# Hybrid attention block: output product fed by transposed raw rows, norms applied on the way out

## The reference, cut to what matters

```python
proj = rms_norm(x, attn_norm) @ w_in
y_nsa = rms_norm(nsa_mixer(...), nsa_out_norm)        # 512 columns, one root per token
o = rms_norm(o, out_gain) * silu(g)                   # HGRN: 4 heads of 128, one root per token and head
x = x + concatenate([y_nsa, y_hg]) @ w_out
h = rms_norm(x, mlp_norm)                             # 1024 columns, one root per token
x = x + square(relu(h @ w_mlp_in)) @ w_mlp_out
```

## Time and profile before

| | us |
|---|---|
| median of 3 runs | 1640.95 |
| range of the runs | 1636.74 to 1642.53 |
| the profiled execution, its own time | 1642.76 |
| its span, first to last instruction | 1640.9 |
| TensorE busy | 1543.2 (94%) |
| VectorE busy | 727.7 (44%) |
| ScalarE busy | 397.9 (24%) |
| GpSimd busy | 423.3 (26%) |
| mean granted TensorE clock | 0.978 |

### The profile page before, as it was taken

The page is one execution under the profiler, slowest core; times in us unless marked ns, Lnnn a source line. Parts: engine busy times, 40 slices in busy tenths (PEclk is TensorE's granted clock), DMA queues, the critical chain, the costliest instruction groups (busy, mean ns, idle before and its releaser), DMA issues.

```text
span 1640.9 us, 24059 instructions
## 1 busy us (share of the span) xinstructions
PE 1543.2 (94%) x8345; PEld 1316.1 (80%) x8345; DVE 727.7 (44%) x1324; ACT 397.9 (24%) x890; POOL 423.3 (26%) x427
## 2 busy tenths in 40 slices
PE   3999998989999999989799699999999999999998
PEld 3988887878888888879688588888888888888886
DVE  5001852016666666689701634444334444334334
ACT  5012311124545454532701411111100111111110
POOL 1333331320000000000323053334444443334411
PEclk9999999998999998999999899999999999999999
DMA  4211130100000000040011021111111111111102
GB/s 151 58 52 45 52 91 24 39 6 1 2 0 0 0 0 0 0 149 2 27 39 59 19 65 45 46 52 52 51 51 51 51 49 47 45 51 51 45 20 103
DMA packets 44690, 69.30 MB, mean 42 GB/s; under 512 B 5688, under 2 KB 23648, under 8 KB 44640
## 3 DMA queue, kind: packets, MB, share of 16 engines
q1 hardware_dynamic: 42368, 67.78, 13.4%
q10 hardware_dynamic: 2272, 0.84, 0.2%
HBM read 64.41 MB, written 4.19 MB: 42 GB/s over the span
## 4 chain that ended last, share of the span: by engine, by line
PE 87%; DVE 8%; ACT 3%; issue 2%; ACTq 0%; DVEq 0%
PE ps L425 65%; PE ps L1517 7%; PE ps L1477 4%; PE ps L1492 4%; PE ps L1540 2%; DVE hT_low L484 1%; PE ps L1511 1%; PE ps L1461 1%; PE ps L1375 1%; PE ps L1482 1%; DVE hgrn_k L1214 1%; PE ps L558 1%; DVE mixed_rows L1303 1%; DVE x L1332 1%; DVE hgrn_q L1213 0%
## 5 line engine op out<-in xcount | busy, mean ns | idle before, releaser
L425 PE MATMUL ps<-hT_high,w_high 128*128 128x512 f32 x640 | 249.1, 389 | 1.4 <-DVE hT_low L484 1.4
L425 PE MATMUL ps<-hT_high,w_low 128*128 128x512 f32 x640 | 249.0, 389 | 0.0
L425 PE MATMUL ps<-hT_low,w_high 128*128 128x512 f32 x640 | 249.0, 389 | 0.0
L1332 DVE TENSOR_TENSOR x<-ps,x 128x512 f32<-128x512 f32 x256 | 171.1, 688 | 97.0 <-PE ps L425 97.0
L742 POOL CAST w_high<-w_raw 128x512 fp32r<-128x512 f32 x128 | 91.6, 716 | 447.5 <-PE ps L425 385.8
L425 PE MATMUL ps<-w_high,hidden_high 128*128 128x512 f32 x512 | 199.4, 390 | 1.6 <-DVE x L1332 1.6
L425 PE MATMUL ps<-w_low,hidden_high 128*128 128x512 f32 x512 | 199.2, 389 | 0.0
L425 PE MATMUL ps<-w_high,hidden_low 128*128 128x512 f32 x512 | 199.2, 389 | 0.0
L1314 DVE TENSOR_TENSOR relu_squared<-relu 128x512 f32<-128x512 f32 x64 | 49.2, 791 | 322.3 <-ACT relu L970 322.3
L970 ACT ACTIVATE relu<-ps 128x512 f32<-128x512 f32 x64 | 38.4, 600 | 589.4 <-PE ps L425 587.9
L744 POOL TENSOR_TENSOR w_low<-w_raw,w_high 128x512 fp32r<-128x512 f32 x128 | 174.5, 1363 | 10.2
(11 more groups left out here) (175 smaller groups left out, 2237.1 us busy)
## 6 DMA issues: line engine op xcount, KB each, us to landing
w_raw<-in_w_mlp_in_dram SPq DMA_DIRECT2D x64, 256.0 KB, 2.7
w_raw<-in_w_mlp_out_dram SPq DMA_DIRECT2D x64, 256.0 KB, 2.8
w_raw<-in_w_in_dram SPq DMA_DIRECT2D x48, 256.0 KB, 2.7
x_in<-in_x_dram SPq DMA_DIRECT2D x8, 512.0 KB, 8.8
w_raw<-in_w_out_dram SPq DMA_DIRECT2D x16, 256.0 KB, 2.8
x<-in_x_dram SPq DMA_DIRECT2D x8, 512.0 KB, 7.3
out_dram<-x SPq DMA_DIRECT2D x8, 512.0 KB, 3.6
w_raw<-in_w_in_dram SPq DMA_DIRECT2D x8, 140.0 KB, 7.2
```

The source lines that it names most:

```text
L425: ins = nc.tensor.matmul(out_ap, a_hl[i], b_hl[j], start=first and n == 0, stop=last and n == 2)
L1332: dve.tensor_tensor(xs, ps[:, (0 if g == 2 else 4) + tt, :], xs, ALU.add).then_inc(res_out, 1)
```

## The change

The rows are no longer scaled before they are transposed.

- The attention output is transposed raw. Its gain sits in `ycol`, one value per partition of the transposed tile, and is applied as ScalarE's scale and as VectorE's scalar when the copies leave PSUM (`fill_act`, `fill_dve`). Its root, a scalar of a token, is applied where the product leaves PSUM and is added to the residual (`add_unit`).
- The HGRN rows are multiplied by root and gate in one instruction per head (`out_rows`); the gain is `ocol`. ScalarE squares all four heads in one instruction and VectorE sums them (`output_sums`). The gate multiply on GpSimd is gone.
- The MLP's rows are transposed raw, with the gain in `g2col`; the root squared is applied in every residual addition of the MLP, since relu and square let a positive row factor through.
- The product is cut into 8 units of 4 chunks by 4 token tiles, 48 matmuls each, on banks 4 to 7 and 0 to 3 in turn (`mix_pe`). Units 0 to 3 take the attention half of the weights, 4 to 7 the HGRN half. Chunks 4 to 7 and 12 to 15 of `w_out` are split into `w2_high` and `w2_low`.
- 16 transposes at a time (`fill_pe`) stand behind scan chunks 4 and 5 (attention), in the middle of units 1 and 2 (HGRN), of units 5 to 7 and behind the first quarter of the first hidden product (residual sums). The squares for the MLP's root now run beside the first hidden product.
- The last key product of the scan and the eighth `kT` are gone. Three constants are added, `ycol`, `ocol` and `g2col`, loaded with single elements next to each other in no dimension: 1664 elements of 4 bytes.

```diff
+    def fill_pe(N, bank0, source):
+        for f in range(4):
+            for q in range(4):
+                ins = nc.tensor.transpose(ps[:, bank0 + f, q * P:(q + 1) * P], source(f, q), eye[:])
+            ins.then_inc(rowsT_done, 1)
+    def fill_act(act, N, bank0, high, gain):
+        for f in range(4):
+            act.wait_ge(rowsT_done, N + f + 1)
+            act.activation(high(f), ps[:, bank0 + f, :], ACT.Copy, scale=gain(f)).then_inc(rows_high, 1)
+    def fill_dve(dve, N, bank0, high, low, gain):
+        for f in range(4):
+            dve.wait_ge(rows_high, N + f + 1)
+            dve.scalar_tensor_tensor(low(f), ps[:, bank0 + f, :], gain(f), high(f).bitcast(F32), ALU.mult, ALU.subtract)\
+                .then_inc(rows_low, 1)
...
-            for c in range(NT):
-                pool.tensor_tensor(per_head(hv[:, 1, c, :]), per_head(hv[:, 1, c, :]),
-                                   hgain.unsqueeze(1).to_broadcast([P, HH, P]), ALU.mult).then_inc(gt_ready, 1)
-            for j in range(16):
-                split_chunk(pool, W_OUT_AT, W_OUT_AT // RING, j)
+            for m in range(16):
+                if m == 4:
+                    pool.wait_ge(O_full, NT)
+                    pool.wait_ge(rowsT_done, Y_AT + 8)
+                split_to(*((w_high, w_low), (w2_high, w2_low))[(m // 4) % 2], W_OUT_AT + m - m % 4, W_OUT_AT // RING + m // 4,
+                         m % 4, W_OUT_AT + m - m % 4 - 8 if m >= 8 else None)
...
+            for dst, src in ((ycol[:], nsa_out_norm[0].rearrange("(k p) -> p k", p=P)),
+                             (ocol[:], hgrn_out_norm[0].rearrange("(k p) -> p k", p=P)),
+                             (g2col[:], mlp_norm[0].rearrange("(k p) -> p k", p=P))):
+                act.dma_start(dst, src, allow_slow_non_contiguous=True).then_inc(c_loaded, 16)
...
-                        for t in range(4):
-                            y_rows(4 * grp + t)
...
+            def output_sums(c):
+                dve.wait_ge(osq_ready, c + 1)
+                dve.tensor_reduce(ssq[:, NT + HH * c:NT + HH * (c + 1)].unsqueeze(2), osq[c % 2], AX, ALU.add).then_inc(osum_ready, 1)
...
+            output_sums(NT - 2)
+            root_dve(dve, cols_of(NT, NT + 4 * HH), P)
+            for t in range(4):
+                dve.wait_ge(ho_out, t + 1)
+                out_rows(t)
+            output_sums(NT - 1)
+            root_dve(dve, cols_of(NT + 4 * HH, NT + 8 * HH), P)
+            for t in range(4, NT):
+                dve.wait_ge(ho_out, t + 1)
+                out_rows(t)
+            dve.wait_ge(x2_loaded, 16 * NT)
+            for u in range(8):
+                add_unit(u)
...
+            def fill_o(tg):
+                pe.wait_ge(rows_ready, NT + 4 * tg + 4)
+                pe.wait_ge(res_out, 4 * tg + 4)
+                fill_pe(O_AT + 4 * tg, 4 - 4 * tg, lambda f, q: hv[:, 0, 4 * tg + q, f * P:(f + 1) * P])
+            pe.wait_ge(rows_low, Y_AT + 8)
+            mix_pe(0)
...
+            mix_pe(1, lambda: fill_o(0))
```

More of the change, by code:

```diff
@@ new lines, in first_hidden_act @@
+            def first_hidden_act(half):
+                for c in range(2):
+                    n = 2 * half + c
+                    b = 2 * c + half
+                    if n < 3:
+                        act.wait_ge(m1_full, n + 1)
+                    else:
+                        act.wait_ge(w_used, hidden_chunk(0) + RING)
+                    act.activation(relu[:, b, :], ps[:, 4 + b, :], ACT.Relu).then_inc(m1_out, 1)
+                    act.wait_ge(m1_out, n + 1)
+                    act.activation(h1_H[:, 0, c, half * BW:(half + 1) * BW], relu[:, b, :], ACT.Square).then_inc(h_high, 1)
@@ L955, in _ @@
+            for half in range(2):
+                squares2(half)
+                first_hidden_act(half)
             act.wait_ge(sums_ready, NT + 1)
             root_act(act, cols_of(48, 48 + NT), D)
-            for t in range(NT):
-                high_rows(act, 2, t)
             def hidden_act(i, par, c):
@@ L1339, in block_dve @@
                     add_group(i, g)
-            for c in range(2):
-                hidden_dve(0, 0, c)
             with dve.Fori(0, NFB // 2 - 1) as r:
@@ L1590, in _ @@
             for c in range(NT):
[L1591 removed]
+                if c < 3:
                     kT(c + 4)
[L1593 to L1600 removed]
@@ new lines, in _, with mix_pe @@
+                outputs(c)
+                if c in (4, 5):
+                    fill_y(c - 4)
+            def mix_pe(u, middle=None):
+                part, blk, tg, b0 = mix_unit(u)
+                hi, lo = ((w_high, w_low), (w2_high, w2_low))[(u // 2) % 2]
+                for k in range(4):
+                    m = 4 * (u // 2) + k
+                    pe.wait_ge(w_split, W_OUT_AT + m + 1)
+                    for tt in range(4):
+                        t = 4 * tg + tt
+                        a = [h[:, 4 * part + k, t * P:(t + 1) * P] for h in (HT_H, HT_L)]
+                        ins = three_passes(ps[:, b0 + tt, :], a, [w[:, k, :] for w in (hi, lo)], k == 0, k == 3)
+                        if tg == 1 and tt == 3:
+                            ins.then_inc(w_used, 1)
+                        elif k == 3:
+                            ins.then_inc(wo_full, 1)
+                    if k == 1 and middle:
+                        middle()
@@ L1627, in hidden_pe @@
+            first_hidden_pe(0, 0)
+            fill_x1(3)
+            first_hidden_pe(1, 0)
+            pe.wait_ge(rows_low, X_AT + 16)
+            for c in range(2):
+                first_hidden_pe(c, 1)
             def hidden_pe(i, c):
@@ L1681, in block_pe @@
                 group_pe(i, par, 3, last)
-            for c in range(2):
-                hidden_pe(0, c)
             for i in range(2):
```

289 lines of the change are left out of this document (158 added, 131 removed).

## The result

The changed kernel takes 1619.09 us (median of 4, 1615.88 to 1621.13) against 1641.42 (1636.74 to 1642.53) for the kernel before: a ratio of 0.9866, interval 0.984 to 0.9893. That is 22.3 us less; 22.5 were predicted (1618.5 us). The profiled execution has a span of 1614.1 us and a time of 1615.88, the shortest of the four, so the two profiles stand 26.9 us apart. How much of this is chance has to be known before any term is compared. In experiment 10 one execution of six took 3908.97 us, in a slow state, and is left out of the numbers given there.

What follows compares the result with a forecast made beforehand. Bound: TensorE's own work plus the seams. 36.3 saved, less 8.9 (new wait), 2.0 (clock), 2.5 (start) and 0.4 (joints), gives 22.5 us less: 1618.5 us on the median, range 1607 to 1629.

Steps and rivals of the forecast that it cites:

- Bound and sum: TensorE's own work plus seams sets the time; the first hidden product ends 36.3 us earlier, at 921.3, not 957.6.
- Scan and first seam: End of scan: TensorE's work with waits of 0.4 and 1.05 us takes 12.1; product starts at 801.75, not 820.88.
- Tree levels: Without eight root-and-gain multiplies on VectorE the scan starts 1.6 us earlier, ends 0 and 2.7.
- The new wait: Middle of unit 1: TensorE waits 8.9 us for the first four residual additions; ends 1.2 and 12.
- Rival (1): HGRN rows pass between GpSimd's splits: wait 1.2 us, clock kept, total 1608.8 us; chance 0.22.
- The turns: VectorE's HGRN rows and GpSimd's splits alternate by whole instructions; first 16 rows end at 814.1, not 808.7.
- Clock: The wait in unit 1 brings back the lower clock: 2.0 us lost, ends 0 and 4.
- Start: Three added constant loads delay VectorE's first instruction, and everything up to the first matmul, by 2.5 us; ends 1.5 and 8.
- the sign named for it: In the changed profile, VectorE's first instruction stands near 20.5 us, against 18.06 before.
- Later units and MLP adds: Six later copy sets hide behind 5.4 us of matmuls each; the MLP's 256 multiply-adds cost nothing.
- (4): Slower than before: at 0.3 us per single element the loads at the start cost 31 us, total 1647; chance 0.03.
- (5): Transposes inside the product wait for VectorE as long as at the seams, some 17 us more, 1636; chance 0.03.

Runs made afterwards that it cites:

- experiment 10: Kernel of experiment 9, with VectorE making the scan's last state between the second and third low halves of the attention rows: 1604.53 us, ratio 0.978.
- Experiment 6: Changed kernel with eight 128x512 multiplies put back on VectorE in the last tree level: 1619.92 us, ratio 0.9877 to the kernel before.
- Experiment 7: Changed kernel with GpSimd's splitting of weight chunks 4 to 7 held back until VectorE has made all HGRN rows: 1610.19 us, ratio 0.9794.
- experiment 8: Changed kernel with unit 0's residual additions ahead of VectorE's second root and second 16 rows, GpSimd left as it was: 1608.24 us, ratio 0.9784.
- experiments 2 and 3: Kernel before plus the three gain-column loads: 1645.03 us; changed kernel with those loads issued later, behind ScalarE's last normed-row copy: 1616.16 us, repeated 1612.03.
- experiment 11: Changed kernel with the MLP's 256 residual additions as plain additions, row root left out: 1619.89 us, ratio 0.9856.
- experiment 5: Changed kernel with the three gain-column loads issued ahead of ScalarE's twelve constants, not behind them: 1625.58 us, ratio 0.9902.
- experiment 9: Changed kernel with unit 0's additions ahead of the second rows and the gain-column loads issued later: 1604.56 us, ratio 0.9762.

## Why the prediction was right, step by step

- **Bound and sum.** TensorE's work plus seams held: behind the MLP's first output both kernels take 665.7 to 665.8 us, so all of the change lies ahead of it.
- **Scan and first seam.** Scan to product was worked out as 801.75 - 775.3 = 26.4 us; 26.22. The waits of 0.4 and 1.05 us are 0.3 and 0.81.
- **Tree levels.** 1.6 us; in the profile 2.1 (77.14 to 75.00), by the median of eleven executions 1.5, single ones 0.4 to 3.1. Experiment 6 confirms the direction, not the size; 1.05 us of it repeat in every trace, as two shorter waits.
- **The new wait.** 8.9 us; 8.45, at the place named. Its parts were right as well: the chain alone ends 17.2 us behind the product's start (predicted 819.3 - 801.75 = 17.6), and leaves a wait of 0.78 (1.2). Experiment 7 shows that GpSimd makes the other 7.7 us, experiment 8 that the order on VectorE's queue lets it reach TensorE. Rival (1), that the rows pass between the splits, falls; its numbers come out only with GpSimd silent. The turns were half right. Beside GpSimd one row passes for each GpSimd instruction, as the prediction had it (four rows to 809.4 us), but only VectorE pays: GpSimd's subtraction stays at 1.29 us (1.27 alone). The Trainium skill, SBUF — State Buffer, section Who interferes with whom, makes contention for the shared ports an exclusive lock. The rows agree: a row issued with a subtraction of 1.29 us took 1.45, and 0.34 alone. The same section of the Trainium skill says that a TENSOR_SCALAR can contend too, when it runs in a mode that uses both port pairs. I had counted only instructions with two inputs, and the root's TENSOR_SCALAR took 0.78 us in place of 0.17 (experiment 7); that it was in such a mode no trace shows. The prediction reached 803.5 with some 1.5 us of copy and square for which it names no row. The step held: VectorE's root was to start 803.5 - 801.75 = 1.75 us behind the product's start, and in experiment 7 it does so 1.7 us behind it.
- **Clock.** 2.0 us. From the first of the sixteen transposes behind the wait to the third matmul after them TensorE took 4.21 us (826.04 to 830.25), at the next set 2.22 (840.73 to 842.95): 2.0 lost. Experiment 7 agrees: it is worth 9.7 us, of which the wait accounts for 7.7. The size is partly luck: the prediction read 10 matmuls at 0.43 us out of a row of 3.5 us; in the trace of before eight of them started 0.42 to 0.43 apart, and the first 16 lost 1.7 us.
- **Start.** This is the step that failed. The 2.5 us were a landing time, with ScalarE's issues hidden. Measured are 5.06 in the profile and 4.7 between the medians of the table (47.05 with the loads in place, 42.34 without). By the trace's landing records the last constant arrived at 19.80 us (18.04 before), and VectorE's first instruction waited until 20.61 for ScalarE's root; what cost was ScalarE held in the issue, and its squares stand on the path of the start. So the sign named for it, VectorE's first instruction near 20.5, came out for another reason than the one given, which is luck. The range had 1.5 to 8 for another reason as well. The estimate of 1.1 us, from the packet figure of the Trainium skill, DMA: Bandwidth & Descriptors, section Bandwidth (about 10.5 ns), was off further, since it too priced the landing; besides, the Trainium skill gives that figure for the 64 packets of one transfer together, and the prediction laid it on each engine's 104. The Trainium skill's rule in DMA: Bandwidth & Descriptors, section Rules for kernel authors, is one descriptor per element for a non-contiguous last dimension. The trace agrees: ScalarE's queue carried 2272 packets before and 3984 after, 1712 more for 1664 elements. A price for them showed only at the busy start (experiments 2 and 3).
- **Later units and MLP adds.** No wait at the transposes of units 5 to 7; the additions cost nothing (experiment 11).

So the total is right partly by offset, which is luck: the start cost 2.2 to 2.6 more than predicted, and scan to MLP gave 24.4 where the terms sum to 36.3 - 1.6 - 8.9 - 2.0 - 0.4 = 23.4. Without chance in attention and projections the measured terms add to 24.4 + 1.5 - 4.7 = 21.2 us, within the measured 17.6 to 26.3. The chances had a slip of their own: all but (4) and half of (5) is 0.955, not 0.94.

## What to carry to other kernels

When work is moved under a long product, follow each wait of the product back through the queue of the engine that ends it: here four additions stood behind a second root and 16 row instructions that the product did not need yet, and another order was worth 10 us, more than half of what the change had brought between scan and product (43.97 to 26.22). Hold back a helper engine that has time when it reads SBUF beside the engine on the path (9.7 us for one wait). And price a load of many small pieces by the issuing engine's time as well as by its landing: issue it at a moment when few transfers are under way, as at 40 us here. An engine that nobody waits for could issue it too, which no run here tried.

## What the runs showed of the hardware

- A DMA issue can hold its engine. The same three loads of 1664 elements took 0.39, 2.06 and 2.58 us to issue behind twelve constants, 0.39, 0.52 and 0.39 alone at 40 us, and ahead of the constants they passed the stall on to an ordinary load, 9.77 us. That the issue waits for room on its queue is my reading; how much room there is was not measured, and whether the queue or the busy DMA engines set it stays open (experiment 5).
- Beside GpSimd's casts and subtractions it was VectorE that was slowed at this place: 16 row instructions of 128 columns from 4.29 to 7.14 us, a TENSOR_SCALAR of 16 columns from 0.17 to 0.78 and once, in experiment 9, to 1.28, GpSimd's subtraction from 1.27 to 1.29. One of 1.61 in the kernel before shows that GpSimd can lose too.
- The same attention stage takes 326.0 to 326.5 us in six executions and 329.5 to 331.8 in eight, with differing granted clock, and one kernel showed both. These up to 5.8 us are 0.36% of 1620, about the size of the prediction's 0.3%. What makes the clock differ was not found.
